# Product-key routing: one wide comparison and one late sum a head, earlier key scores, and dense numbers looked up tile by tile

## What is computed

```python
q = (hf @ w_q).reshape(T, PEER_HEADS, 2, PEER_HALF)
s1 = jnp.einsum('thd,hkd->thk', q[:, :, 0], sub_keys[:, 0])
s2 = jnp.einsum('thd,hkd->thk', q[:, :, 1], sub_keys[:, 1])
v1, i1 = lax.top_k(s1, PEER_TOPK)
v2, i2 = lax.top_k(s2, PEER_TOPK)
cand = (v1[..., :, None] + v2[..., None, :]).reshape(T, PEER_HEADS, PEER_TOPK * PEER_TOPK)
sc, ci = lax.top_k(cand, PEER_TOPK)
e = (jnp.take_along_axis(i1, ci // PEER_TOPK, axis=-1) * N_KEYS
     + jnp.take_along_axis(i2, ci % PEER_TOPK, axis=-1))
g = jax.nn.softmax(sc.astype(jnp.float32), axis=-1).astype(h.dtype)
# per token: sum over its 128 (t, k) of gelu(x . u_tab[e]) * g * v_tab[e]
```

## Time and profile before

| | |
|---|---|
| Median of 3 runs | 1890.51 us (1882.92 to 1895.56) |
| The profiled execution's own time | 1890.23 us |
| Its span | 1888.4 us |
| Mean granted TensorE clock | 0.958 of 2.4 GHz |
| PE busy | 1723.7 us (91%) |
| VectorE busy | 1567.8 us (83%) |
| ACT busy | 743.8 us (39%) |
| GpSimd busy | 684.6 us (36%) |
| Chain that ended last | VectorE 36%, DMA 21%, PE 20%, issue 19% |

### The profile page before, as it was taken

One profiled execution on the slowest core, in us unless ns is written; L12 is line 12 of the kernel. 1 busy time (PEld: TensorE's weight loads), 2 busy tenths in 40 slices (PEclk: granted clock), 3 DMA queues, 4 the chain that ended last, 5 costly groups with the idle time before them and its releaser, 6 DMA issues.

```text
span 1888.4 us, 28707 instructions
## 1 busy us (share of the span) xinstructions
PE 1723.7 (91%) x9208; PEld 1406.5 (74%) x9208; DVE 1567.8 (83%) x3196; ACT 743.8 (39%) x1615; POOL 684.6 (36%) x616
## 2 busy tenths in 40 slices
PE   6999798989776288789999999999999999999997
PEld 4655674546444177678889989999998999999986
DVE  2693861138999799789999999999999999999998
ACT  3111462020001188744444444444444444444443
POOL 0000000003545688634444444443444444443441
PEclk9999899999887589999999999999999999999999
DMA  7443101111110247899999999999999999999996
GB/s 313 146 156 104 42 1 59 56 40 50 44 44 22 89 135 222 268 390 387 395 393 397 411 388 406 407 401 403 390 408 383 408 410 392 412 399 403 398 393 216
DMA packets 128780, 509.05 MB, mean 270 GB/s; under 512 B 8528, under 2 KB 63568, under 8 KB 79184
## 3 DMA queue, kind: packets, MB, share of 16 engines
q0 software_dynamic: 36864, 268.45, 35.3%
q1 hardware_dynamic: 91568, 239.69, 33.9%
q10 hardware_dynamic: 288, 0.13, 0.0%
HBM read 480.32 MB, written 27.92 MB: 269 GB/s over the span
## 4 chain that ended last, share of the span: by engine, by line
DVE 36%; DMA 21%; PE 20%; issue 19%; POOL 2%; DVEq 1%; ACT 1%; POOLq 0%; SPq 0%; ACTq 0%
DMA slab<-table,ixr 21%; PE psum L403 11%; DVE slab L1284 8%; DVE ulo L1226 4%; DVE slab L1247 3%; PE psum L404 3%; DVE slab L1276 2%; DVE vlo L1263 2%; PE psum L653 2%; DVE slab L1271 2%; POOL slab L1361 1%; DVE wlo L1259 1%; DVE slab L999 1%; DVE slab L1251 1%; DVE slab L1196 1%
## 5 line engine op out<-in xcount | busy, mean ns | idle before, releaser
L1361 POOL DMA_INDIRECT slab<-table,ixr x256 | 425.6, 1662 | 604.8 <-DVE slab L1284 555.0
L403 PE MATMUL psum<-slab 128*128 128x512 f32 x624 | 329.9, 611 | 19.9 <-ACT slab L722 10.9
L674 PE MATMUL psum<-hhi,uhi 128*128 128x384 f32 x1008 | 339.6, 337 | 7.1 <-issue 7.1
L1284 DVE SCALAR_TENSOR_TENSOR slab<-slab,cf 128x1024 f32<-128x1024 f32 x256 | 328.2, 1282 | 14.7
L1276 DVE SCALAR_TENSOR_TENSOR slab<-slab,h2tok 128x1024 f32<-128x1024 f32 x256 | 312.1, 1219 | 32.7 <-DMA slab<-table,ixr 32.5
L674 PE MATMUL psum<-hhi,ulo 128*128 128x384 f32 x1008 | 338.4, 336 | 0.0
L674 PE MATMUL psum<-hlo,uhi 128*128 128x384 f32 x1008 | 337.8, 335 | 0.0
L688 PE MATMUL psum<-vhi,whi 128*128 128x512 f32 x768 | 299.9, 391 | 13.8 <-DVE wlo L1259 13.8
L688 PE MATMUL psum<-vhi,wlo 128*128 128x512 f32 x768 | 302.3, 394 | 0.0
L688 PE MATMUL psum<-vlo,whi 128*128 128x512 f32 x768 | 302.2, 394 | 0.0
L404 PEld LDWEIGHTS psum<-slab 128*128 128x128 f32 x624 | 120.9, 194 | 154.3 <-issue 154.3
(11 more groups left out here) (177 smaller groups left out, 2554.8 us busy)
## 6 DMA issues: line engine op xcount, KB each, us to landing
slab<-ublk SPq DMA_DIRECT2D x64, 1024.0 KB, 9.0
slab<-vtab SPq DMA_DIRECT2D x64, 1024.0 KB, 9.0
slab<-wblk SPq DMA_DIRECT2D x90, 512.0 KB, 4.7
slab<-g_dram SPq DMA_DIRECT2D x32, 768.0 KB, 9.5
g_dram<-slab SPq DMA_DIRECT2D x11, 2048.0 KB, 8.9
slab<-table,ixr POOLq DMA_INDIRECT x256, 9.9
x<-x_in SPq DMA_DIRECT2D x1, 2560.0 KB, 10.2
y_out<-x SPq DMA_DIRECT2D x5, 512.0 KB, 4.1
```

The source lines that it names most:

```text
L403: pe.matmul(dst[:, 0:512], w, src[:, l0:l0 + T_L], start=start, stop=stop)
L674: last = pe.matmul(psum[:, b, 0:ND], w[:, c, :], m[:, c, :], start=(m_ == 0), stop=(m_ == 3 * DC - 1))
L1284: v.scalar_tensor_tensor(out=accs[k][:, e, :], in0=rows[:, sl % GR, D:2 * D], scalar=cf[:, sl:sl + 1], in1=accs[k][:, e, :], op0=ALU.mult, ...
L1361: pool.indirect_dma_start(out=rows[:, sl % GR, :], out_offset=None, in_=table, in_offset=bass.IndirectOffsetOnAxis(ap=ixr[:, half, sl % 8: ...
```

## The change

**The comparison.** `place`, `hit` and `count` are laid out with the 16 places inside the 50 candidates. `count` is repeated 16 times in SBUF. The five comparisons of a head are one instruction over 4000 elements, and `found` counts heads.

**The numbers.** GpSimd adds once more: 50 to 25 to 13 candidates (`FOLD`), three instructions a tile. VectorE's five sums are one over 5 x 16 x 13 elements, and it stands behind the shift of the scores, ahead of `topf`, where before it stood behind `ranked`.

**Key scores.** Scores 0 and 1 are issued right behind their own query blocks, none behind block 2, scores 2 behind block 3. In the loops nothing changes.

**Splits.** `hhi` is copied right behind the last shift and `hlo` is made ahead of the first search.

**The last head's numbers.** GpSimd's loop ends one head earlier; for the last head it does only the two gather tiles, into a buffer of their own (`hit_last`). VectorE multiplies and sums the three dense tiles itself (`tried_numbers`, `dense_numbers`) around `den` and `gw`. PE waits for each tile (`dense_looked`). `slot_number` releases the split into key indices once the number is copied. The gather tiles' last sum, their `idxu` and the two `ulo` stand behind the first dense tile's 32 steps. ACT makes its two `uhi` copies ahead of the exponential.

```diff
+FOLD = CAND // 4 + 1
...
-        hit = view(13824, TILES, TOP, CAND)
+        hit = view(13824, TILES, CAND, TOP)
...
+        hit_last = view(35712, N_GATHER, CAND, TOP)
...
+        count = view(19248, CAND * TOP // 2).bitcast(BF16).rearrange("p (n k) -> p n k", n=CAND)
...
                     linear(lin[j % 2], weights(S_WQ + j, None if first else i), h, fresh=DC if first and j == 0 else None)
-                    if not first or j:
+                    if first and j < 2:
+                        key_scores(j)
+                    elif not first or j > 2:
                         key_scores(j - 1, None if first else i)
...
             for k in range(N_DENSE):
                 pe.wait_ge(picked, 1)
+                pe.wait_ge(dense_looked, k + 1)
...
             act.wait_ge(kv_stored, 32)
+            act.wait_ge(h_ready, 2 * DC)
+            act.copy(hhi[:], h[:, :, 0:ND]).then_inc(hsplit, 1)
...
-            act.copy(hhi[:], h[:, :, 0:ND]).then_inc(hsplit, 1)
...
-            act.wait_ge(shifted, 1)
-            act.activation(ex, ex, ACT.Exp).then_inc(exped, 1)
...
             for n in range(2):
                 u_lead(n, n, True)
+            act.wait_ge(shifted, 1)
+            act.activation(ex, ex, ACT.Exp).then_inc(exped, 1)
...
             rms_scale(1, 4)
+            v.wait_ge(scaled, 2 * DC)
+            v.wait_ge(hsplit, 1)
+            v.tensor_tensor(hlo[:], h[:, :, 0:ND], hhi[:].bitcast(F32), ALU.subtract).then_inc(hsplit, 1)
...
             def numbers(i):
 
-                for t in range(TILES):
-                    v.wait_ge(folded, i * TILES + (t + 1 - TILES))
-                    v.tensor_reduce(ef[:, t, bass.ds((i - 1) * TOP, TOP)], hit[:, t, :, 0:CAND // 2], AX_X, ALU.add).then_inc(looked, 1)
+                v.wait_ge(folded, i * TILES)
+                v.tensor_reduce(ef[:, :, bass.ds((i - 1) * TOP, TOP)], hit[:, :, 0:FOLD, :].rearrange("p t n k -> p t k n"), AX_X, ALU.add).then_inc(looked, 1)
...
                 v.sem_inc(ranked, 1)
-                if not first:
-                    numbers(i)
...
                 if not first:
+                    numbers(i)
                     v.wait_ge(valued, i * TILES)
-                    v.wait_ge(looked, i * TILES)
+                    v.wait_ge(looked, i)
                 tk(v.tensor_copy(topf[:], topi[:]))
                 own()
 
-                for t in range(TILES):
-                    v.tensor_tensor(place[:, t], count[:].unsqueeze(1).broadcast_to([P, TOP, CAND]),
-                                    topf[:, t, :].unsqueeze(2).broadcast_to([P, TOP, CAND]), ALU.is_equal).then_inc(found, 1)
+                each = [P, TILES, CAND, TOP]
+                v.tensor_tensor(place, count.unsqueeze(1).broadcast_to(each), topf[:].unsqueeze(2).broadcast_to(each), ALU.is_equal).then_inc(found, 1)
...
+            def tried_numbers(k):
+
+                t = N_GATHER + k
+                v.tensor_tensor(hit[:, t], place[:, t], eid[:, t, :].unsqueeze(2).broadcast_to([P, CAND, TOP]), ALU.mult).then_inc(tried, 1)
+
+            def dense_numbers(k):
+
+                t = N_GATHER + k
+                v.wait_ge(tried, k + 1)
+                v.tensor_reduce(ef[:, t, (PH - 1) * TOP:PH * TOP], hit[:, t].rearrange("p n k -> p k n"), AX_X, ALU.add).then_inc(dense_looked, 1)
...
+                if k == 0:
+                    v.wait_ge(folded, TILES * (PH - 1) + N_GATHER)
+                    v.tensor_reduce(ef[:, 0:N_GATHER, (PH - 1) * TOP:PH * TOP], hit_last[:, :, 0:FOLD, :].rearrange("p t n k -> p t k n"), AX_X, ALU.add)\
+                        .then_inc(looked, 1)
+                    v.wait_ge(looked, PH)
+                    step(v.tensor_copy(idxu[:, 0:N_GATHER], ef[:, 0:N_GATHER]))
+                    settle()
+                    for n in range(2):
+                        u_rest(n, n)
...
-                for t in range(TILES):
-                    pool.tensor_tensor(hit[:, t], place[:, t], eid[:, t, :].unsqueeze(1).broadcast_to([P, TOP, CAND]), ALU.mult).then_inc(valued, 1)
+                pool.wait_ge(found, i + 1)
+                for t in range(tiles):
+                    pool.tensor_tensor(hit[:, t], place[:, t], eid[:, t, :].unsqueeze(2).broadcast_to([P, CAND, TOP]), ALU.mult).then_inc(valued, 1)
                     pool.wait_ge(valued, i * TILES + (t + 1))
-                    pool.tensor_tensor(hit[:, t, :, 0:CAND // 2], hit[:, t, :, 0:CAND // 2], hit[:, t, :, CAND // 2:CAND], ALU.add).then_inc(folded, 1)
+                    pool.tensor_tensor(hit[:, t, 0:CAND // 2], hit[:, t, 0:CAND // 2], hit[:, t, CAND // 2:CAND], ALU.add).then_inc(halved, 1)
+                    pool.wait_ge(halved, i * TILES + (t + 1))
+                    pool.tensor_tensor(hit[:, t, 0:FOLD - 1], hit[:, t, 0:FOLD - 1], hit[:, t, FOLD:CAND // 2], ALU.add).then_inc(folded, 1)
+            with pool.Fori(0, PH - 1) as i:
+                look_up(i, TILES, hit)
+            look_up(PH - 1, N_GATHER, hit_last)
```

More of the change, by code:

```diff
@@ L154, in build @@
         topf = sb("topf", [P, TILES, TOP], BF16)
-        count = sb("count", [P, CAND], BF16)
         den = sb("den", [P, TILES * PH])
@@ L202, in build @@
         scr = view(25344, 2, TILES, P)
-        hit = view(13824, TILES, TOP, CAND)
-        place = view(22784, TILES * TOP * CAND // 2).bitcast(BF16).rearrange("p (t k n) -> p t k n", t=TILES, k=TOP)
-        cand, cand2, eid = view(17824, TILES, CAND), view(18080, TILES, CAND), view(18336, TILES, CAND)
+        hit = view(13824, TILES, CAND, TOP)
+        place = view(22784, TILES * TOP * CAND // 2).bitcast(BF16).rearrange("p (t n k) -> p t n k", t=TILES, n=CAND)
+        cand, cand2, eid = view(17824, TILES, CAND), view(18080, TILES, CAND), view(35456, TILES, CAND)
+        hit_last = view(35712, N_GATHER, CAND, TOP)
         ex = view(18608, TILES, PH, TOP)
+        count = view(19248, CAND * TOP // 2).bitcast(BF16).rearrange("p (n k) -> p n k", n=CAND)
         accs = (view(9216, 2, D), view(23552, 2, D))
@@ L853, in _ @@
                 act.wait_ge(by_slot, k + 1)
-                act.copy(eT[:, t * P:(t + 1) * P], psum[:, k, 0:P])
+                act.copy(eT[:, t * P:(t + 1) * P], psum[:, k, 0:P]).then_inc(slot_number, 1)
                 act.copy(gT[:, t * P:(t + 1) * P], psum[:, k, P:2 * P])
@@ L1189, in search @@
                 if not first:
+                    numbers(i)
                     v.wait_ge(valued, i * TILES)
[L1191 removed]
+                    v.wait_ge(looked, i)
                 tk(v.tensor_copy(topf[:], topi[:]))
                 own()
[L1195 to L1197 removed]
+                each = [P, TILES, CAND, TOP]
+                v.tensor_tensor(place, count.unsqueeze(1).broadcast_to(each), topf[:].unsqueeze(2).broadcast_to(each), ALU.is_equal).then_inc(found, 1)
                 assert k[0] == HEAD_STEPS
[L1200 removed]
+            v.tensor_copy(count, con[:, C_IOTA:C_IOTA + CAND].unsqueeze(2).broadcast_to([P, CAND, TOP])).then_inc(topk_step, 1)
             search(0, True)
@@ L1205, in _, with u_rest @@
             v.sem_inc(shifted, 1)
-            v.wait_ge(hsplit, 1)
-            v.tensor_tensor(hlo[:], h[:, :, 0:ND], hhi[:].bitcast(F32), ALU.subtract).then_inc(hsplit, 1)
-            numbers(PH)
+            def tried_numbers(k):
[5 more added lines that the diff above has]
+                v.tensor_reduce(ef[:, t, (PH - 1) * TOP:PH * TOP], hit[:, t].rearrange("p n k -> p k n"), AX_X, ALU.add).then_inc(dense_looked, 1)
+            def u_rest(n, jj):
+                v.wait_ge(uhi_set, n + 1)
+                v.tensor_tensor(ulo[:, jj % 4], uraw[:, jj // 2 % 2, jj % 2], uhi[:, jj % 2].bitcast(F32), ALU.subtract).then_inc(ulo_set, 1)
+            exh = ex.rearrange("p t h k -> p (t h) k")
+            v.wait_ge(found, PH)
+            v.wait_ge(number_step, PH * NUMBER_STEPS)
+            v.wait_ge(looked, PH - 1)
+            tried_numbers(0)
             v.wait_ge(exped, 1)
-            exh = ex.rearrange("p t h k -> p (t h) k")
             step(v.tensor_reduce(den[:], exh, AX_X, ALU.add))
-            v.wait_ge(looked, TILES * PH)
-            step(v.tensor_copy(idxu[:], ef[:]))
+            dense_numbers(0)
             settle()
             step(v.reciprocal(den[:], den[:]))
+            tried_numbers(1)
             settle()
@@ L1220, in _ @@
                 .then_inc(picked, 1)
+            dense_numbers(1)
+            tried_numbers(2)
             read_mod(2 + N_MID, 6, N_ADA3, M_G2)
-            def u_rest(n, jj):
-                v.wait_ge(uhi_set, n + 1)
-                v.tensor_tensor(ulo[:, jj % 4], uraw[:, jj // 2 % 2, jj % 2], uhi[:, jj % 2].bitcast(F32), ALU.subtract).then_inc(ulo_set, 1)
-            for n in range(2):
-                u_rest(n, n)
+            dense_numbers(2)
             for k in range(N_DENSE):
@@ L1241, in _ @@
                 v.sem_inc(halves_set, 1)
+                v.wait_ge(slot_set, k + 1)
                 for b in range(k * P // 4, (k + 1) * P // 4):
@@ L1324, in _, with look_up @@
```

(2 more changed lines are left out.)

8 lines of the change are left out of this document (3 added, 5 removed).

## The result

The changed kernel takes 1876.19 us (median, 1873.86 to 1881.69), the kernel before 1892.5 us on the same chip. The medians lie 16 us apart. The ratio over all runs, by which the kernels are compared here, is 0.9929, 95% interval 0.9915 to 0.9942: 13 us faster, about half of the 25.4 forecast. Run once more beside the later experiments it gave 0.9931 (0.9914 to 0.9948), 13 us again. It lies just inside the wider range of 1857 to 1877, but that is luck, for the range was stretched for a comparison at 4.3 us, and the comparison took 2.24.

A forecast was written before the change was run, and what follows sets the result against it. VectorE was taken to bound the one-hot stage and every head, with engines waiting in turn in the tail. First one-hot 29.1 us earlier, less 3.7 returning, gives 25.4: 1865 us; own range 1857 to 1871, wider 1857 to 1877.

The forecast's parts named there:

- a comparison at 4.3 us: Rival: each head's comparison on VectorE stays at one element a clock, 4.3 us; 1876 us in all; chance 0.17.
- the comparison: One VectorE instruction of 4000 elements a head instead of five taking 4.60 us: 2.5 us, so -2.05 us a head.
- The start: First query block to head 1 on VectorE: halves at 417.2, 427.0, 445.7 and 455.7 us; hlo costs nothing.
- the 2.7 us: Gain kept behind the start: head 1's second half at 455.7 us, where it began at 458.4 before.
- The head: Loop over heads on VectorE: net -2.55 us a head, period 24.7 us instead of 27.25.
- The late sum: VectorE's one sum over 1040 elements a head: 1.23 us and 0.1 for a wait, +1.35 us a head.
- The collisions: Seven candidate instructions on VectorE meet GpSimd's instructions four times a head: +0.75 us; lower bound none, upper 2.4 us.
- Slow sums: Rival: sums stepping 64 bytes double their time per element; 9.3 us lost, 1874 us; chance 0.15 together with full collisions.
- full collisions: Rival: VectorE waits out all four meetings, 2.4 us a head; costs 9.9 us, 1875 us; chance 0.15 together with slow sums.
- The tail: From PE's release at 608.0 us to the first one-hot at 636.05 instead of 665.18, 29.1 us earlier.
- The 3.7 us behind the first dense tile: Sum, cast, two ulo and waits come back on VectorE behind the first dense tile: +3.7 us.
- become the bound: Rival: GpSimd's products slow down, at 4.3 us each a head lasts 33.3 us; 1921 us in all; chance 0.04.

The follow-up runs named there:

- the run with the pause: The changed kernel, but GpSimd holds back each head's last of five tiles until VectorE's seven candidate additions of the next head are done: 1865.97 us, ratio 0.9866.

## Why the prediction failed, step by step

**The start: right.** Forecast for VectorE's halves were 417.2, 427.0, 445.7 and 455.7 us; measured are 416.75, 427.48, 446.00 and 455.68. hlo cost nothing there. What I did not see is whose gain the 2.7 us were: with the scores in the old place head 1's second half starts at the same time, so they came from head 0, whose comparison is 2.36 us shorter.

**The head: wrong in two terms.** In the sum of -2.55 us a head the comparison was taken at 2.5 us and took 2.24 (-0.26). The Trainium skill ("VectorE: DVE Perf Modes", the perf-mode tier table) gives two elements a cycle for a tensor_tensor on bfloat16 in SBUF; an estimate from that page's figures makes 2.25 us of it. The measurement agrees. The late sum was taken at 1.23 us by the rate of sums over neighbours, and took 1.92 (+0.69). The collisions were taken at 0.75 us and took 2.35 (+1.60), the upper bound that I had worked out. Together +2.03: a period of 26.7, measured 26.8. Over heads 2 to 6 this makes 10 us of the 10.7 by which PE's release missed (618.73 instead of 608.0).

The step that failed is the choice between the bounds of the collisions. I took the price of head 0, where seven additions met one cast of 0.33 us and lost 0.19, and multiplied by four meetings. But the four meetings are with the last 1.1 us of a product, additions of 1.03 and 0.59 us, and then the cast, and each was waited out. GpSimd's first product beside hlo (4.70 us) had shown that a wait lasts as long as the other's instruction; I cited it for the upper bound and then left it. The Trainium skill ("SBUF — State Buffer", "SBUF: two separate sides") says that a VectorE instruction with two SBUF inputs and a GpSimd instruction that reads SBUF lock each other out for a whole instruction. The trace agrees: each of the four long additions ended with the GpSimd instruction that it had met. By that rule the term is the prediction's own upper bound, 2.4 us a head.

**The rivals: apart, where they belonged together.** Slow sums and full collisions each had a price (9.3 and 9.9 us), and both came true, the sums at two thirds of a doubling. They have different causes, so they add: by the measured sizes the forecast becomes 1865 + 8.0 for the collisions (5 x 1.60) + 4.1 for the sums (6 x 0.69) + 1.5 for three dense sums (1.42 us from start to start instead of 0.9) - 1.6 for the comparison (6 x 0.26), 1877 us.

**The tail: right but for the dense sums and one more collision.** From PE's release to the first one-hot it is 29.5 us where 39.1 stood before: 9.7 gained, 11.1 forecast. Of the tail's edits only the exponential's place was taken back by itself, so how the 9.7 divide among the others is not shown. From PE's release to u's issue 11.2 us (11.1 forecast), to the den sum 20.1 (20.15). VectorE waited 3.17 us there (about 4). From the den sum to the first one-hot it was 9.35 us instead of 7.9. The three strided sums make 1.5 of it. The rest nearly cancels: `gw` took 1.21 us beside a GpSimd addition (642.26 us), where in the run with the pause, without one beside it, it took 0.81, and the small terms came out shorter than forecast. The 3.7 us behind the first dense tile were 3.5 (688.07 to 691.56).

**Behind it: right.** 17.0 - 3.5 = 13.5 us; the first vlo moved by 13.0, and the ratio of the times makes 13 too (the medians lie 16 apart). GpSimd did not become the bound (a product takes 1.57 us, not 3.4), and the expert steps kept their time.

## What to carry to other kernels

When work is shortened on one engine, look at what of another engine slides beside it: short two-operand VectorE instructions next to GpSimd's reads of SBUF can wait for the end of a GpSimd instruction again and again (four of seven here), and a single wait on the engine that has slack is the cure. Count such a meeting at what is left of the GpSimd instruction met, not at a price seen with a shorter one. Before elements are laid out for one fast instruction, price the reader at the other end: here the new layout gave the comparison 2.1 us a head and took 0.7 from the sum.

## What the runs showed of the hardware

- A float32 sum on VectorE runs at 1.23 us for 1040 elements at steps of 4 and 8 bytes and at 1.92 to 2.03 us from 16 to 256 bytes.
- A comparison of two bfloat16 operands takes 2.24 us for 4000 elements with inner steps of one, though one operand has a zero step in its outer dimension and the other in its middle one, and 4.33 us when one operand's inner step is zero.
- Beside a GpSimd memset, whose row has no input, two integer tensor_scalar instructions of VectorE with one input took 1.85 and 1.78 us, and 0.22 when the memset stood elsewhere. A dense sum of the changed kernel beside the same memset (643.39 us) kept its 1.50 us.
- A plain increment of a semaphore does not wait for the instruction ahead of it: `shifted`, which stands behind the last comparison in VectorE's program, released ACT 0.3 us after that comparison had started (632.20 and 632.50), 1.9 us before it ended.
